# A streaming hybrid encoder step on one core: the expert outputs are combined and the final norm is made with tokens on partitions, and the squares of the two middle norms are summed as they arise

## The reference

```python
for l in range(DEPTH):                      # DEPTH = 1
    h = rmsnorm(x, P['g_mix'][l]) * (1 + sc1) + sh1
    m, ns = mixer(h, st_l, P, l, lb_all[l]) # SSD, HGRN2 and S5 heads, out_a = rmsnorm(y_a, ssd_norm_g)
    x = x + gt1 * m                         # m = merged @ w_out
    h = rmsnorm(x, P['g_ffn'][l]) * (1 + sc2) + sh2
    x = x + gt2 * hmoe(h, P, l)             # 32 experts, two per token, weighted
y = rmsnorm(x, P['g_final'])
```

## Time and profile before

| | us |
|---|---|
| median of 3 runs | 1496.92 |
| lowest, highest | 1494.64, 1498.01 |
| profiled execution, its own time | 1496.93 |
| its span | 1495.0 |
| span, the share with TensorE busy | 82% |
| span, the share with VectorE busy | 35% |

### The profile page before, as it was taken

The page is one execution under the profiler, slowest core; times in us unless marked ns, Lnnn a source line. Parts: engine busy times, 40 slices in busy tenths (PEclk is TensorE's granted clock), DMA queues, the critical chain, the costliest instruction groups (busy, mean ns, idle before and its releaser), DMA issues.

```text
span 1495.0 us, 14778 instructions
## 1 busy us (share of the span) xinstructions
PE 1224.5 (82%) x5914; PEld 664.9 (44%) x5914; DVE 520.3 (35%) x1020; ACT 197.6 (13%) x319; POOL 261.6 (18%) x568
## 2 busy tenths in 40 slices
PE   4799999989998778989979768787878777877625
PEld 2346555545555445656657444233323222333224
DVE  1412575644563673246621441111211111111054
ACT  1311011010211310132210320000000000000011
POOL 4170288881000000021120000000001000000010
PEclk9899899989998889899989878999999988999857
DMA  9998668675574636332123526999999999999432
GB/s 341 368 359 301 211 225 281 234 273 172 185 274 159 235 105 234 127 95 91 57 71 121 216 72 243 420 421 417 416 410 391 409 403 416 398 413 409 175 138 71
DMA packets 140085, 387.01 MB, mean 259 GB/s; under 512 B 15211, under 2 KB 54501, under 8 KB 112558
## 3 DMA queue, kind: packets, MB, share of 16 engines
q1 hardware_dynamic: 132208, 361.91, 64.2%
q0 software_dynamic: 6528, 18.72, 3.6%
q10 hardware_dynamic: 1280, 5.42, 1.0%
HBM read 385.95 MB, written 23.13 MB: 274 GB/s over the span
## 4 chain that ended last, share of the span: by engine, by line
PE 45%; DMA 26%; DVE 10%; POOL 10%; issue 3%; ACT 2%; SPq 2%; DVEq 0%; POOLq 0%; ACTq 0%
DMA slot<-in_w_exp_up 21%; PE psum L1411 11%; PE psum L1066 10%; PE psum L1345 5%; PE psum L1099 4%; DMA slot<-in_w_ada 4%; PE psum L995 3%; PE psum L965 2%; PE psum L956 2%; POOL mem L540 2%; POOL sq L541 2%; POOL sq L538 2%; POOL mem L543 2%; POOL sq L542 1%; POOL sq L539 1%
## 5 line engine op out<-in xcount | busy, mean ns | idle before, releaser
L1411 PE MATMUL psum<-slot,mem 128*64 128x512 f32 x1024 | 258.8, 664 | 83.4 <-DMA slot<-in_w_exp_up 82.5
L1066 PE MATMUL psum<-hT,slot 128*128 128x320 f32 (+1 forms) x1056 | 308.3, 452 | 0.0
L1066 PEld LDWEIGHTS psum<-hT,slot 128*128 128x128 f32 (+1 forms) x1056 | 204.5, 196 | 100.3 <-issue 27.9
L1411 PEld LDWEIGHTS psum<-slot,mem 128*64 128x64 f32 x1024 | 85.7, 153 | 255.2 <-issue 171.4
L2128 DVE TENSOR_TENSOR sq<-sq,psum 128x256 f32<-128x256 f32 x16 | 6.7, 422 | 380.7 <-ACT sq L911 380.7
L1435 PE MATMUL psum<-mem,sq 128*64 128x512 f32 x512 | 113.4, 594 | 8.6 <-issue 7.1
L965 PE MATMUL psum<-slot,cT 128*8 128x512 f32 (+1 forms) x768 | 98.9, 629 | 21.1 <-DMA slot<-in_w_ada 20.9
L610 POOL DMA_INDIRECT moe_output<-mem,idx x16 | 16.2, 1011 | 483.6 <-ACT mem L915 483.6
L1345 PE MATMUL psum<-mem,slot 128*128 128x320 f32 x256 | 71.9, 445 | 5.4 <-DVE mem L1954 5.4
L1099 PE MATMUL psum<-mem,slot 128*128 128x320 f32 x256 | 75.2, 450 | 0.0
L1435 PEld LDWEIGHTS psum<-mem,sq 128*64 128x64 f32 x512 | 41.9, 137 | 69.9 <-issue 68.7
(11 more groups left out here) (426 smaller groups left out, 1301.1 us busy)
## 6 DMA issues: line engine op xcount, KB each, us to landing
slot<-in_w_ada SPq DMA_DIRECT2D x48, 2048.0 KB, 11.0
slot<-in_w_exp_gate SPq DMA_DIRECT2D x64, 1024.0 KB, 14.7
slot<-in_w_exp_up SPq DMA_DIRECT2D x64, 1024.0 KB, 16.9
mem<-in_w_exp_down SPq DMA_DIRECT2D x32, 2048.0 KB, 17.5
slot<-in_w_in SPq DMA_DIRECT2D x17, 2048.0 KB, 11.8
slot<-in_w_out SPq DMA_DIRECT2D x8, 2048.0 KB, 8.4
mem<-in_w_in SPq DMA_DIRECT2D x2, 2048.0 KB, 18.4
mem<-in_x_prompt ACTq DMA_DIRECT2D x1, 2048.0 KB, 12.4
```

What stands on the lines that cost most here:

```text
L1066: last = mm(psum[0:wd, grp % 2, 0:T], w[:, k, q * P:q * P + wd], hT[:, k, :], start=(k == 0), stop=(k == KD - 1))
L1411: last = mm(psum[rows_, 0, :].rearrange("p (w n) -> p w n", w=2), xe[i % 2][:, k, rows_], gate_up[h][:, :, k, :], start=(k == 0), stop=(k ...
```

## The change

It has four parts. In the **SSD stage** and its norm, ScalarE squares each chunk as soon as it is done, into `hT`, which is free by then; TensorE sums the squares of the 256 prompt columns before the last chunk's products, and those of the last chunk after it.

```diff
+            def chunk_squares(c):
+
+                cols = slice(c * CH, c * CH + CH)
+                act.wait_ge(S("ssd_done"), c + 1)
+                st(s.activation(hT[:, 0:8, cols], proj[:, 0:8, cols], ACT.Square), "squares")
...
+                if c:
+                    chunk_squares(c - 1)
...
+                if c == NCH - 1:
+                    pe.wait_ge(S("squares"), NORM["ssd"] + 4)
+                    for k in range(8):
+                        last = mm(bank(2, TP), ones[:, :], hT[:, k, 0:TP], start=(k == 0), stop=(k == 7))
+                    last.then_inc(S("squares_used"), 4)
...
-                    sum_squares(3, 4, "ssd")
+                    pe.wait_ge(S("squares"), NORM["ssd"] + 5)
+                    for k in range(8):
+                        last = mm(bank(2, TS, lo=TP), ones[:, :], hT[:, k, TP:T], start=(k == 0), stop=(k == 7))
```

```diff
-            sum_squares(3, 8, "n2")
+            pe.wait_ge(S("squares_used"), NORM["n2"] + 7)
+            for q in range(2):
+                mm(bank(3, T), ones[:, :], sum_sq[:, q * T:q * T + T], start=(q == 0), stop=False)
+            pe.wait_ge(S("squares"), NORM["n2"] + 8)
+            for q in range(2):
+                last = mm(bank(3, T), ones[:, :], sq[:, 1, q * T:q * T + T], start=False, stop=(q == 1))
...
+                if m % 2 and m > 1:
+                    i = m // 2 - 1
+                    dve.wait_ge(S("squares"), NORM["n2"] + i + 1)
+                    if i == 0:
+                        st(v.tensor_copy(sum_sq, sq[:, 0, :]), "squares_used", wait=False)
+                    else:
+                        dve.wait_ge(S("squares_used"), NORM["n2"] + i)
+                        st(tt(sum_sq, sum_sq, sq[:, i % 2, :], ADD), "squares_used", wait=False)
...
-            modulate(g_ffn, 4)
-            for k in range(KD):
-                shift_sample(3, k)
+            for k, n in ((0, 1), (1, 1), (2, 2), (4, 4), (8, 4), (12, 4)):
+                scale_x(k, n)
+                for kk in range(k, k + n):
+                    shift_sample(3, kk)
```

```diff
-                b3 = hb3(hb, m)
-                st(tt(hb3(hE, m), b3, bc(b3[:, :, m - 1:m], [P, 640 // (2 * m), 2 * m]), SUB))
-                st(stt(hE, hE, -1.0, hE, MUL, ALU.min), "hg_expo")
+                early, later = (slice(0, m), slice(m, 2 * m))
+                b3, e3 = hb3(hb, m), hb3(hE, m)
+                ref = bc(b3[:, :, m - 1:m], [P, 640 // (2 * m), m])
+                st(tt(e3[:, :, later], b3[:, :, later], ref, SUB), wait=False)
+                st(tt(e3[:, :, early], ref, b3[:, :, early], SUB), "hg_expo")
...
-                st(tt(hq_, q_, hE, MUL))
-                st(tt(hk_, k_, hE, MUL), "hg_qk")
+                st(tt(hb3(hq_, m)[:, :, later], hb3(q_, m)[:, :, later], e3[:, :, later], MUL), wait=False)
+                st(tt(hb3(hk_, m)[:, :, early], hb3(k_, m)[:, :, early], e3[:, :, early], MUL), "hg_qk")
```

```diff
+ROWS_AT = [1 + n // 2 for n in range(20)] + [NPAIR - 2] * 4
...
+                pe.wait_ge(S("xe_ready"), 4 * XE_DONE[n])
+                if n >= 2:
+                    pe.wait_ge(S("nat_taken"), n - 1)
+                b = 6 + n % 2
+                if n < 12:
+                    j, kg = n // 4, n % 4
+                    w = P if j < 2 else TS
+                    for q in range(4):
+                        last = tr(bank(b, P, w, lo=q * P), xT[:, 4 * kg + q, j * P:j * P + w], ident[:, :])
+                else:
+                    kg = n % 4
+                    col = (seg(5)[:, :, 0:1], g_fin.unsqueeze(2), seg(5)[:, :, 1:2])[(n - 12) // 4]
+                    for q in range(4):
+                        last = mm(bank(b, P, lo=q * P), bc(col[:, 4 * kg + q, :], [P, P]), ident[:, :], start=True, stop=True)
+                last.then_inc(S("nat_turned"), 1)
...
+                for n in range(24):
+                    if ROWS_AT[n] == i:
+                        dve.wait_ge(S("nat_turned"), n + 1)
+                        cols = slice(512 * (n % 4), 512 * (n % 4) + 512)
+                        into = (x_nat + [gt2_rows[0], g_rows, gt2_rows[2]])[n // 4]
+                        w = TS if n // 4 == 2 else P
+                        v.tensor_copy(into[0:w, cols], bank(6 + n % 2, 512, w)).then_inc(S("nat_taken"), 1)
```

```diff
-            pool.wait_ge(S("down_done"), 2 * NPAIR)
+            pool.wait_ge(S("x_final"), 1)
...
+            def square_sum(j):
...
+                act.wait_ge(S("z_ready"), j + 1)
+                s.activation(r2[0:n, j, :], r1[0:n, j, :], ACT.Square, accum_out=rt[0:n, 480 + j:481 + j])\
+                 .then_inc(S("z_squared"), 1)
...
+            def std(j):
...
+                act.wait_ge(S("mean_square"), 4 + j)
+                s.activation(rt[0:n, 484 + j:485 + j], rt[0:n, 484 + j:485 + j], ACT.Sqrt).then_inc(S("root"), 1)
...
+            weigh(0)
+            weigh(1)
+            square_sum(0)
+            weigh(2)
+            std(0)
+            square_sum(1)
+            std(1)
+            square_sum(2)
+            std(2)
...
+            def weigh_sum(j):
...
+                dve.wait_ge(S("act_rows"), 12 + j + 1)
+                st(stt(r1[0:n, j, :], r2[0:n, j, :], wk[0:n, 3 + j:4 + j], r1[0:n, j, :], MUL, ADD))
...
+            def gate_add(j):
...
+                st(tt(r1[0:n, j, :], r1[0:n, j, :], gt2_rows[j][0:n, :], MUL))
+                st(tt(r1[0:n, j, :], r1[0:n, j, :], x_nat[j][0:n, :], ADD), "z_ready")
...
+            def variance(j):
...
+                dve.wait_ge(S("z_squared"), j + 1)
+                st(ts(rt[0:n, 484 + j:485 + j], rt[0:n, 480 + j:481 + j], 1.0 / D, EPS, MUL, ADD), "mean_square")
...
+            def normalize(j):
...
+                dve.wait_ge(S("root"), 4 + j)
+                st(v.reciprocal(rt[0:n, 488 + j:489 + j], rt[0:n, 484 + j:485 + j]))
+                st(stt(r1[0:n, j, :], r1[0:n, j, :], rt[0:n, 488 + j:489 + j], g_rows[0:n, :], MUL, MUL), "y_rows", wait=False)
...
+            weigh_sum(0)
+            gate_add(0)
+            weigh_sum(1)
+            variance(0)
+            gate_add(1)
+            normalize(0)
+            weigh_sum(2)
+            variance(1)
+            gate_add(2)
+            normalize(1)
+            variance(2)
+            normalize(2)
```

210 lines of the change are left out of this document (105 added, 105 removed).

## The result

The changed kernel takes 1447.01 us (median of 4 runs, 1444.56 to 1447.30), the kernel before, beside it, 1495.78 (4 runs, 1494.16 to 1498.01): a ratio of 0.9669, 95% interval 0.9651 to 0.9687. Forecast were 1445.6 and a range of 1437 to 1454. The profiled execution took 1447.30 with a span of 1445.6, against 1496.93 and 1495.0 before, so 49.4 us of span are to be explained; the prediction's sum was 51.3.

What follows compares the result with a forecast made beforehand. The bound differs by stage: DMA in the expert stage, a serial chain in the tail, mostly TensorE in HGRN2. Gains 30.4 + 0.5 + 5.0 + 11.1 + 4.3 = 51.3 us give 1445.6 us, range 1437 to 1454.

Steps and rivals of the forecast that it cites:

- The tail: From VectorE's first sum to the last store's issue: new row layout makes the last store 30.4 us earlier (29.1 to 31).
- The new wait: Gathers before the tail now wait for `x_final` instead of `down_done`; claimed cost 0.
- The cost in the expert stage: Inserted turns, 2.2 us of TensorE in each of pairs 1 to 10, cost 0; uncovered, 22 us.
- Pair 14/15: Last expert pairs: first half 3.0 us later, second half waits 2.3; gain 0.5 us (bounds 0 and 2.1).
- Norm of the SSD output: After SSD's last chunk: VectorE starts on the norm's sum 5.0 us earlier (3.4 to 5.5).
- n2 and the router: Norm n2 through router matmuls: gains of 5.0, 0.8 and 5.3 us, together 11.1 (2.8 to 12.1).
- HGRN2's levels: HGRN2: instructions of 320 columns instead of 640 shorten four TensorE waits by 4.3 us in all; lower bound 0.
- The lower clock stayed in the router's matmuls: Rival: lower clock stays there, or n2's sum falls to it; 3 to 8 us lost, 1451; chance 0.15.
- longer: Rival, expert stage: inserted turns lengthen each pair, 22 us more and the 0.5 lost, 1468; chance 0.06.
- shorter pairs: Rival, expert stage: less waiting keeps TensorE at 2.4 GHz, 20 us less, 1426; chance 0.05.
- `turn_x` waited for no copy: Rival, expert stage: `turn_x` waits for late copies, stalling TensorE and loads; at 6 us per pair, 1506; chance 0.01.
- The middle delivered: Denies the rival that norms and levels gain nothing because another wait ends as late: 1466; chance 0.05.

Runs made afterwards that it cites:

- tail_only: The kernel before with only the change's expert-stage and tail part; 1465.06 us (4 runs), ratio 0.9806 to the kernel before.
- middle_only: The kernel before with only the change's HGRN2 levels, SSD norm, n2 sum and scaling/shift pieces; 1475.01 us, ratio 0.9876 to the kernel before.
- undo_levels: The changed kernel with HGRN2's levels as before, in four instructions of 640 columns; 1444.42 us (one run).
- changed_again: The changed kernel unaltered, timed again beside the one with filled waits; 1445.36 us (4 runs), ratio 0.9661 to the kernel before.
- the nine-fold run: The changed kernel with the turns of the first 20 groups in the expert stage made nine times; 1466.37 us (one run).

## Why the prediction was right, step by step

**The tail.** Right: 31.05 us between the same two instructions against 30.4, and the order of VectorE's list came as written. The TENSOR_TENSOR takes 2.29, the sum 2.35, ScalarE's pass 1.91 plus 0.19 for the accumulator, where I had 2.30, 2.35 and 2.1. Most of the 0.6 us is my allowance for narrow instructions and hops, 2.0 us where the trace has 1.63 beside 27.8 of wide ones; another 0.3 us came ahead of the first sum. The new way is 29.43 in `tail_only` too, but the old one, with its turns on TensorE, took 59.15 in `middle_only` and not 60.48, so the gain is known to 1.3 us only. The new wait costs 0, as said: `x_final` is there at 1392.97, when the gather goes at 1400.22.

**The cost in the expert stage.** Right in the sum, wrong in a term. I read the row of 1.09 us as four transposes; it is eight. Two groups cost 1.06 in six pairs and 2.05 in the four with matmuls, not 2.2 in ten. It made no difference, since the cover is 8.1 us. I also put the waits of 0.47 and 5.68 us into different pairs; they are those of the first and the second half of one pair, and the argument stays the same.

**Pair 14/15.** The step itself held, the gain did not:

```profile
1377.84 7.09 PE L1462 MATMUL psum<-slot,mem 128*64 128x512 f32 x32 [2.28 <-DMA slot<-in_w_exp_up]
...
1387.68 7.09 PE L1486 MATMUL psum<-mem,sq 128*64 128x512 f32 x32 [1.38 <-DMA mem<-in_w_exp_down]
```

The second half waits 2.28, as forecast 2.3, and takes 7.09 instead of 9.16: that is 2.07 gained, the upper bound. But then the down product waits 1.38 us for its weights. These are issued at 1364.59, behind the weights of the second half (1354.09 to 1355.41), and their landing had been hidden by the slow half; the kernel before has no wait for them there. The next late thing is `in_w_exp_down`, and I hadn't looked for it. Whether 0.5 us was gained or 0.65 lost in the whole stage can't be told: from the first down product to the last it is 483.27 and 482.64 us in two traces of the changed kernel, and 482.62 and 481.90 with the old stage (before, `middle_only`).

**Norm of the SSD output.** 5.33 against 5.0. The inserted 3.72 us cost 0.26 and not 0.5 at the last piece. They replace a wait of 1.47, and the products and the piece behind run at the high clock, 1.10, 1.15 and 4.57 against 1.34, 1.97 and 5.07. The 0.27 us of a transpose, by which I bounded the eight matmuls of 64 columns, came from the same misreading and is half of that; the eight took 2.0 us where I had 1.8.

**n2 and the router.** The sum of squares was right to 0.01 (4.99), and the router's matmuls end 12.93 us after scaling starts against 13.0. The stretch before n2 gave 1.1 us that I hadn't in the sum; the projection's matmuls take 70.8 us instead of 71.9. Both follow a wait of 5.43 us, and the clock came back later behind it in the kernel before; nothing in the change was meant to do that.

**HGRN2's levels.** The waits give 4.3 as forecast, the stretch gave 5.90, 1.4 more than the bound of 4.5. The rest is the clock, in both directions. 10.57 us behind the wait of 3.06 became 8.88 behind the wait of 1.49, which is 1.69, and the lead is 4.06 us at the last level of the first pair of heads. At the first level of the second pair it is 3.14, since the lower clock stayed longer behind the next long wait, and only later stretches bring it to 5.90. In nine traces with the new levels the stretch takes 360.2 to 364.7 us, so its gain beyond 4.3 is luck of the trace. I had read waits on TensorE as costing their own length. They cost their length and, behind it, from nothing (8.88 us behind 3.06 in `undo_levels`) to 2.4 us and more (11.26 behind 13.18 in `changed_again`).

**The rivals.** The lower clock stayed in the router's matmuls, at 11.64 against 11.77, as the forecast itself kept it. Neither longer nor shorter pairs came. `turn_x` waited for no copy, even with nine times the turns. The middle delivered.

**The total.** 1445.6 against 1447.0 is closer than the terms deserve: 3.1 us of better terms met 4.9 us of a late front, and neither was foreseen. That much of it is luck.

## What to carry to other kernels

Where a wait of TensorE can't be removed, fill it with matmuls of constants into a bank that is about to be overwritten: ten such places gave 13.5 us, more than a quarter of what this whole change gave. Before you add work to a stage, measure its slack by doing the work several times over: the nine-fold run here gave both the cover and the price beyond it. Compare stretches between two instructions rather than whole times when a term is smaller than the scatter, and ask of every wait that shrinks what was landing behind it.

## What the runs showed that I had not expected

What a wait of TensorE leaves behind it is no constant: the same matmuls took 10.57 or 8.88 us behind 3.06 us of wait, and 11.77, 10.31 or 10.08 behind 10.86. With the waits filled the mean granted clock of the run rose from 0.909 to 0.928. VectorE and GpSimd exclude each other for whole instructions where VectorE's has two inputs in SBUF, 4.50 us at a time in the tail. TensorE's course behind the first sigmoid is remarkably even: nine traces with the new levels have the same three instructions within 0.02 us of 30.88, 55.20 and 83.24 after the sigmoid, and go apart by up to 3 us behind the next long wait.
